# A two-block transformer kernel in float32: the state steps of its RWKV part put in another order

## The reference, cut to what matters

```python
def step(S, inp):
    w_t, k_t, v_t, a_t, b_t = inp[:5]
    sa = jnp.einsum('bhij,bhj->bhi', S, a_t)
    S = S * w_t[:, :, None, :] + sa[..., None] * b_t[:, :, None, :] + v_t[..., None] * k_t[:, :, None, :]
    y = jnp.einsum('bhij,bhj->bhi', S, inp[5]) if emit else None
    return S, y
```

## Time and profile before

| | us |
|---|---|
| median of 3 runs | 2797.05 (2795.35 to 2806.27) |
| profiled execution | 2801.67 |
| its span in the profile | 2799.5 |
| TensorE busy, all of the span | 2506.8 |
| VectorE busy | 894.2 |
| ScalarE busy | 534.8 |
| GpSimd busy | 153.5 |
| mean granted clock of TensorE | 0.937 of full |

### The profile page before, as it was taken

The page is one execution under the profiler, slowest core; times in us unless marked ns, Lnnn a source line. Parts: engine busy times, 40 slices in busy tenths (PEclk is TensorE's granted clock), DMA queues, the critical chain, the costliest instruction groups (busy, mean ns, idle before and its releaser), DMA issues.

```text
span 2799.5 us, 36794 instructions
## 1 busy us (share of the span) xinstructions
PE 2506.8 (90%) x15530; PEld 1778.1 (64%) x15530; DVE 894.2 (32%) x1608; ACT 534.8 (19%) x1067; POOL 153.5 (5%) x145
## 2 busy tenths in 40 slices
PE   8999989999999899999989999999767777777786
PEld 6857678887857788887568888864333343333333
DVE  3733524203725412313575651231111111111112
ACT  2125310001126212002234422121000000000002
POOL 1310000000310000000011110100000000000000
PEclk9999999999999999999999999999888878888778
DMA  8336547545331473453000002559999999999998
GB/s 330 141 135 256 210 181 267 215 151 210 121 144 67 151 273 121 191 230 117 1 1 2 1 2 104 210 203 428 427 427 429 428 428 429 428 429 429 428 429 359
DMA packets 48772, 666.89 MB, mean 238 GB/s; under 512 B 5530, under 2 KB 5573, under 8 KB 7568
## 3 DMA queue, kind: packets, MB, share of 16 engines
q1 hardware_dynamic: 46928, 657.81, 57.7%
q0 software_dynamic: 1728, 7.38, 0.8%
HBM read 664.11 MB, written 1.05 MB: 238 GB/s over the span
## 4 chain that ended last, share of the span: by engine, by line
PE 63%; DMA 27%; DVE 7%; ACT 2%; issue 1%; POOL 0%; DVEq 0%; SPq 0%; ACTq 0%
PE bank L2689 50%; DMA ring<-exp_w 25%; PE bank L2697 6%; PE bank L2701 2%; PE bank L2919 2%; DVE arena L2422 1%; PE bank L1884 1%; DMA ring<-w_in 1%; DVE hT L2566 1%; PE bank L2725 1%; PE bank L1912 1%; DMA arena<-exp_w 1%; ACT arena L2348 0%; PE bank L2939 0%; DVE ring L1441 0%
## 5 line engine op out<-in xcount | busy, mean ns | idle before, releaser
L2689 PE MATMUL bank<-hT,ring 128*128 128x256 f32 (+2 forms) x3232 | 735.2, 387 | 5.2 <-ACT hT L2222 4.0
L2689 PEld LDWEIGHTS bank<-hT,ring 128*128 128x128 f32 x3232 | 603.5, 191 | 139.9 <-issue 63.6
L2697 PE MATMUL bank<-ring,arena 128*32 128x512 f32 (+1 forms) x2496 | 320.9, 655 | 170.6 <-DMA ring<-exp_w 156.9
L2689 PE MATMUL bank<-arena,ring 128*128 128x256 f32 x1600 | 352.7, 381 | 7.1 <-POOL arena L2189 2.8
L2689 PEld LDWEIGHTS bank<-arena,ring 128*128 128x128 f32 x1600 | 304.8, 191 | 50.5 <-POOL arena L2189 3.6
L2697 PEld LDWEIGHTS bank<-ring,arena 128*32 128x32 f32 x2496 | 86.8, 128 | 356.8 <-issue 200.3
L2689 PEld LDWEIGHTS bank<-vec,arena 128*128 128x128 f32 x1344 | 173.2, 208 | 73.2 <-issue 68.4
L2689 PE MATMUL bank<-arena 64*128 64x128 f32 (+4 forms) x1156 | 205.2, 375 | 4.6 <-DVE ring L1441 1.6
L1625 DVE COPY arena<-bank 128x512 f32<-128x512 f32 x64 | 44.3, 692 | 477.9 <-PE bank L2697 477.9
L2697 PE MATMUL bank<-arena 128*32 128x256 f32 (+1 forms) x1568 | 156.7, 541 | 42.0 <-DMA arena<-exp_w 41.5
L2689 PE MATMUL bank<-vec,arena 128*128 128x32 f32 (+2 forms) x1344 | 178.6, 284 | 3.4 <-DVE arena L2422 3.4
(11 more groups left out here) (323 smaller groups left out, 2048.7 us busy)
## 6 DMA issues: line engine op xcount, KB each, us to landing
ring<-exp_w SPq DMA_DIRECT2D x125, 2048.0 KB, 26.2
arena<-exp_w SPq DMA_DIRECT2D x66, 2048.0 KB, 26.0
ring<-w_in SPq DMA_DIRECT2D x38, 2048.0 KB, 7.8
ring<-ada_w SPq DMA_DIRECT2D x24, 2048.0 KB, 7.9
ring<-w_mlp_up SPq DMA_DIRECT2D x16, 2048.0 KB, 7.8
ring<-w_mlp_down SPq DMA_DIRECT2D x16, 2048.0 KB, 7.9
ring<-mod_w SPq DMA_DIRECT2D x12, 2048.0 KB, 7.8
ring<-w_out SPq DMA_DIRECT2D x6, 2048.0 KB, 7.9
```

Source lines behind the costliest of these rows:

```text
L2689: mm = nc.tensor.matmul(out_, a, b, start=(i == 0), stop=(i == len(pairs) - 1))
L2697: mm = nc.tensor.matmul(o, a, b, start=(i < 4), stop=(i >= len(pairs) - 4))
```

## The change

- `keep_busy` goes from U0 (two products in each second U0 of groups 0 to 2, one in each first U0). In U it now stands in every second step, in that of group 3 too.
- U0 is cut in two: U0a with the eight score products, and U0 with the eight state products, added on top in the same banks. U0a is issued some jobs ahead, in banks taken before their turn (`started_early`).
- Y is cut likewise: Ya (state and RK products) ahead of the wait for U, Y (RB products) behind it. In S the kT products are issued ahead of the wait for U.
- BK of a group moves from the next group's state steps into its own solve, behind levels 3 and 4 (not for group 0). S0 of the first chunk moves to level 4, and U0a and U0 of the first chunk stand ahead of W6.
- lora of the next group moves from behind NT to behind the second spread (not for group 0). Widening stands ahead of Ya, S and Y of the second chunk.
- S stands ahead of Y, and the last Y frees two weight slots in place of the last S.

```diff
     for g in range(4):
-        if old:
-            yield "S0", q, 0
-        if g >= 2:
-            yield "BK", q, 0
+        yield "NT", g, 0
+        yield "NT", g, 1
+        if g == 0:
+            yield "mix", "ctx", 8
+            yield "lora", n
         if g == 1:
             yield "BK", q, 0
-        if old:
-            yield "U0", q, 0
             yield "BK", q, 1
-        if new:
-            yield "pick", g
         if old:
             yield "U", q, 0
+            yield "U0a", q, 1
+            if q >= 2:
+                yield "Ya", q, 0
+            yield "S", q, 0
+            yield "S0", q, 1
+            if q >= 2:
+                yield "Y", q, 0
+        yield "pick", g
+        if old:
+            yield "U0", q, 1
+        yield "spread", g, 0
+        if old:
+            yield "U", q, 1
+        yield "spread", g, 1
+        if old and ahead:
+            yield "lora", n
+        for tile in range(4):
+            yield "widen", g, tile
+        if g == 0:
+            yield "mix", "ctx", 10
         if old:
             if q >= 2:
+                yield "Ya", q, 1
+            yield "S", q, 1
             if q >= 2:
                 yield "Y", q, 1
...
+            if g and lev < 5:
+                yield "BK", g, lev - 3
+            if lev == 4:
+                yield "S0", g, 0
+        yield "U0a", g, 0
+        yield "U0", g, 0
         for ci in range(2):
             yield "W6", g, ci
...
+    yield "U0a", 3, 1
     yield "U", 3, 0
-    yield "Y", 3, 0
+    yield "Ya", 3, 0
     yield "S", 3, 0
     yield "S0", 3, 1
+    yield "Y", 3, 0
     yield "gates2", 0
     yield "U0", 3, 1
     yield "gates2", 1
     yield "U", 3, 1
+    yield "Ya", 3, 1
     yield "gates2", 2
+    yield "S", 3, 1
     yield "Y", 3, 1
-    yield "S", 3, 1
     yield "gates2", 3
...
+            def started_early(key):
+
+                n = jobs.at[key][0]
+                assert done[0] <= n < done[0] + BANKS
+                emptied(pe, jobs.order[n - BANKS])
+                return bank[n % BANKS]
...
+                elif what == "U0a":
+                    vt = values_of(g, at[0])
+                    banks = [started_early(("U0", g, at[0], par)) for par in range(2)]
+                    emptied(pe, ("AK", g, at[0], 1))
+                    for p in range(CT):
+                        for par in range(2):
+                            nc.tensor.matmul(banks[par][:, p * 64:(p + 1) * 64], score_of("AK", 2 * at[0] + par)[:, p],
+                                             vt[:, p, pars[par]], start=(p == 0), stop=False)
                 elif what == "U0":
                     banks = paired(what, g, at[0])
-                    if g < 3 and at[0] == 1:
-                        keep_busy(banks[0], 2)
-                    elif at[0] == 0:
-                        keep_busy(banks[0], 1)
-                    emptied(pe, ("AK", g, at[0], 1))
                     pe.wait_ge(state_scaled, 2 * g + at[0] + 1)
                     for p in range(CT):
+                        mms = [nc.tensor.matmul(banks[par][:, p * 64:(p + 1) * 64], ops[0][pars[par], p, tok],
+                                                state_in[pars[par], p], start=False, stop=(p == CT - 1)) for par in range(2)]
```

More of the change, by code:

```diff
@@ L302, in rwkv_steps @@
     for g in range(4):
-        q, n, new, old = g - 1, g + 1, g < 4, g > 0
+        q, n, old = g - 1, g + 1, g > 0
         ahead = n < 4
-        if old:
-            yield "S0", q, 0
-        if g >= 2:
-            yield "BK", q, 0
-        if new:
[L310 to L315, removed]
+        yield "NT", g, 0
[3 more added lines that the diff above has]
+            yield "lora", n
         if g == 1:
             yield "BK", q, 0
-        if old:
-            yield "U0", q, 0
             yield "BK", q, 1
-        if new:
-            yield "pick", g
         if old:
             yield "U", q, 0
-        if new:
-            yield "spread", g, 0
+            yield "U0a", q, 1
[18 more added lines that the diff above has]
+            yield "mix", "ctx", 10
         if old:
             if q >= 2:
[L329 to L343, removed]
+                yield "Ya", q, 1
+            yield "S", q, 1
             if q >= 2:
                 yield "Y", q, 1
-            yield "S", q, 1
         if ahead:
@@ L571, in second_block @@
                 for par in range(2):
-                    add((what, g, *at, par), "v")
+                    last = (what, g, *at, par) == ("Y", 3, 1, 1)
+                    add((what, g, *at, par), "v", [("hold", 0, 2), ("hold", 0, 3)] if last else [])
             elif what == "U0":
@@ L583, in second_block @@
             elif what == "W" or what == "S":
-                last = (what, g, *at) == ("S", 3, 1)
-                add((what, g, *at), "v", [("hold", 0, 2), ("hold", 0, 3)] if last else [])
+                add((what, g, *at), "v")
             elif what == "XT6":
@@ L1729, in paired, with values_of @@
                 return [start((name, g, ci, par), par) for par in range(2)]
+            def started_early(key):
[3 more added lines that the diff above has]
+                return bank[n % BANKS]
+            def values_of(g, ci):
+                cc, _ = chunk_tokens(g, ci)
+                return ar(R_VT + 1024 * (g // 2), TT, CT, P)[:, cc]
             def gates(i):
@@ L1888, in second_tensor @@
                     b = start((what, g, *at))
-                    if g < 3 and at[0] == 1:
+                    if at[0] == 1:
                         keep_busy(b, 1)
@@ L1897, in second_tensor @@
                     finish(mm)
[L1898 to L1901, removed]
+                elif what == "Ya":
+                    _, tok = chunk_tokens(g, at[0])
+                    vt = values_of(g, at[0])
+                    banks = [started_early(("Y", g, at[0], par)) for par in range(2)]
                     emptied(pe, ("RK", g, at[0], 1))
[L1903 to L1920, removed]
                     for p in range(CT):
@@ L1924, in second_tensor @@
                                 part = pars[par]
-                                a, c = ((btT[:, p, part], solved_u[:, par, p]), (ktT[:, p, part], vt[:, p, part]))[i]
-                                mm = nc.tensor.matmul(b[part, p * 64:(p + 1) * 64], a, c, start=(i == 0), stop=(i == 1))
+                                a, c = ((state_in[part, p], ops[3][part, p, tok]),
+                                        (vt[:, p, part], score_of("RK", 2 * at[0] + par)[:, p]))[i]
+                                nc.tensor.matmul(banks[par][part, p * P:(p + 1) * P], a, c, start=(p == 0 and i == 0), stop=False)
+                elif what == "Y":
+                    banks = paired(what, g, at[0])
+                    emptied(pe, ("U", g, at[0]))
+                    for p in range(CT):
+                        mms = [nc.tensor.matmul(banks[par][pars[par], p * P:(p + 1) * P], solved_u[:, par, p],
+                                                score_of("RB", 2 * at[0] + par)[:, p], start=False,
+                                                stop=(p == CT - 1)) for par in range(2)]
+                    for mm in mms:
+                        finish(mm)
+                elif what == "S":
+                    vt = values_of(g, at[0])
+                    btT, ktT = (turned_operands(at[0])[:, i] for i in range(2))
+                    b = start((what, g, *at))
+                    emptied(pe, ("kT", g, at[0]))
+                    for p in range(CT):
+                        for part in pars:
+                            nc.tensor.matmul(b[part, p * 64:(p + 1) * 64], ktT[:, p, part], vt[:, p, part], start=(p == 0), stop=False)
+                    emptied(pe, ("U", g, at[0]))
+                    for p in range(CT):
+                        for par in range(2):
+                            mm = nc.tensor.matmul(b[pars[par], p * 64:(p + 1) * 64], btT[:, p, pars[par]], solved_u[:, par, p],
+                                                  start=False, stop=(p == CT - 1))
                     finish(mm)
```

14 lines of the change are left out of this document (1 added, 13 removed).

## The result

| | before | after |
|---|---|---|
| median of the runs (us) | 2804.8 (7 runs) | 2785.5 (7 runs) |
| ratio, 95% interval | | 0.9932 (0.9918 to 0.9946) |
| profiled execution | 2801.67 | 2785.61 |
| its span | 2799.5 | 2783.8 |

What follows compares the result with a forecast made beforehand. TensorE's work was taken to bound the RWKV part; keep_busy 8.1, U0 7.0, waits 1.4 and 0.5, less a new wait 1.6, gave 15.4 us won: 2786 us profiled, 2781.6 as median, range 2775 to 2792.5.

Steps and rivals of the forecast that it cites:

- U0 split: Score and state products of U0 run grouped instead of in turn: 0.88 us for each of eight U0, 7.0 us won.
- keep_busy out: Net nine keep_busy products leave TensorE's queue, booked at 0.9 us each: 8.1 us won.
- Where such a product only filled a wait, the wait stays: Caveat on removed keep_busy products: the second U0 waited for the scaled state, and that wait would not go with them.
- The rival that had the clock: Four to six more clock falls at 1.5 us each, leaving a gain of 6 to 9 us; chance 0.20.
- Waits that go: TensorE waits before NT, U0 and Y vanish, 1.4 us; small ones before second U0 and BK, 0.5 us.
- The new wait in group 3: Without lora there, TensorE waits before group 3's widening, right behind the last spread: 1.6 us lost.
- One fall after as before: The sum counts one clock fall with TensorE busy, 1.5 us, in the changed kernel as in the old.
- It is hidden: Second U0's wait for the scaled state, about 1.35 us, is covered by pick, or by Y and pick.
- Margin of the scan behind the sigmoids: On ScalarE, the sigmoids queued behind the moved lora end 0.9 us before the scan's first operation.
- BK in the solve at nothing: BK moved into the solve keeps its turns and evictions and delays no X: no time booked.
- the tail within the transfer: At the end, gates2's weight chunk lands 7.7 us after its request, within 8.5 us of work: fits by 0.7 us.
- Y and S split at nothing: Cutting Y into Ya and Y, and S into halves, keeps the number of alternations: no time booked.

## Why the prediction was right, point by point

The forecast was 15.4 us won; the profiles show 15.7, the runs 19. The median came out at 2785.5 us and not 2781.6, because the kernel before measured 2804.8 over seven runs where the forecast started from 2797.05 over three. The total is right. Not all of its working is, and that the errors cancel is luck.

The clock's part is best seen in all seven kernels of the first experiments:

| order | U0 | keep_busy in U0 | recurrence (us) | of it at 1.2 GHz |
|---|---|---|---|---|
| old | alternating | yes (before) | 333.6 | 17 |
| old | alternating | no | 353.1 | 72 |
| old | grouped | yes | 323.8 | 10 |
| old | grouped | no | 316.6 | 14 |
| new | alternating | no | 350.0 (a long execution) | 68 |
| new | grouped | yes | 323.0 | 10 |
| new | grouped | no (after) | 317.8 | 17 |

- **U0 split, 7.0 us: right, and it was more than a term.** 2.87 against 3.72 us, 6.8 us in eight; the kernel before with this edit alone won 7.5 us. The reading that an alternation has its price was right. The Trainium skill, page TensorEngine Tiling (Array Packing), section Key Properties, says that a change of tiling mode drains the engine; the trace agrees as far as the 0.85 us a U0 goes. That a drain is what the 0.85 us are is not shown.
- **keep_busy out, 8.1 us: right in size, wrong as a term by itself.** The nine products less are 8.6 us from start to start: the products that went cost some 0.95 us each, the ones that stay 0.88, so the 8.5 us that the prediction first read from its rows was nearer than the 8.1 it booked. But the sum added the term as if it were free of the others. Taken out of the kernel before, ten of them cost 18 us instead of giving 8; taken out behind the grouping they give 7.2. The step that failed is the sentence "Where such a product only filled a wait, the wait stays", with its silence on the clock. The rival that had the clock put four to six short falls on the new order, and they did not come. What makes the clock fall is the alternating U0 without keep_busy beside it, in either order: 68 and 72 us at 1.2 GHz, against 10 to 24 in the ten kernels with a grouped one. An alternating U0 in the new order with keep_busy was not run. What of an alternating U0 does it (that its records leave gaps, or which part of the array they use) the runs don't show.
- **Waits that go, 1.4 and 0.5 us: right** (1.4 and 0.3 measured), and the W waits became 0.9 us shorter besides.
- **The new wait in group 3, 1.6 us: right, 1.74. What follows it was missed:** a fall of 2.9 us in Ya, S and Y, in both profiles of the changed kernel.
- **One fall after as before: right only in the sum.** The clock is low for 17 us in either profile. But the fall at 1560 us is gone, the one in group 1 is half as long (3.4 us at 1.2 GHz in place of 6.8), and the new one in group 3 takes 6.8.
- **"It is hidden", of the wait for the scaled state: wrong.** It waited 0.46 and 0.92 us. The 1.35 us that I gave the three operations became 2.7 to 3.1, because GpSimd's additions ran beside them; before, they ran earlier. I had placed the masks against pick and not asked what the additions behind them share. The Trainium skill, page SBUF — State Buffer, section Who interferes with whom, says that a vector instruction with two SBUF inputs contends with a GpSimd instruction that reads SBUF. The trace agrees: 0.80 to 1.37 us with two such inputs in place of 0.43, and 0.42 with one.
- **Margin of the scan behind the sigmoids, 0.9 us: right**, no wait. But S takes over a bank of theirs and waited 0.57 and 0.29 us, which I had not looked up.
- **BK in the solve at nothing, the tail within the transfer: right.** No new wait before W, none before gates2.
- **Y and S split at nothing: right.** Ya, S and Y take 4.75 us at the full clock (group 2), Y and S before took 4.74.
- **The order of the jobs: nearly nothing.** The old order with the grouping and without the products has a recurrence of 316.6 us, the changed kernel 317.8, or 314.9 without its fall. The new order, which is most of the diff, costs 1.2 us as it stands and would be worth 1.7 without the fall. With the two small edits that keep the additions and the last spread out of the way (312.1) it is worth 4.5.

Of the 15.8 us, then: U0's grouping 6.8, the nine products 8.6, waits gone or shorter 2.6 (0.32, 0.31, 0.78, 0.3 before the second U0, 0.9 before W), the fall at 1560 us 1.5. Against them: new waits 4.0 (1.74, 1.38, 0.86) and the fall in group 3 2.9. That makes 12.6. The rest are pieces of work of the same count that take less from start to start: BK 1.1 (0.87 in place of 1.02 us where it stands behind T), W and XT 1.0 (most of it the shorter low stretch in group 1's first XT, 5.29 in place of 6.05), T 0.8 and U 0.4, which closes the sum to 0.1 us. Why T and U are cheaper in their new places I did not test. The sum had left out 1.4 us of waits for the scaled state, 0.9 for the sigmoids' banks and 1.4 of the larger fall in group 3, and it had left out gains of about as much.

## What to carry to other kernels

Two matmul shapes that use the array differently should be issued in two runs, not in turn, and the run that needs nothing new goes ahead of the wait: here that one edit won 7.5 us, and made 7 us of filler products needless. A filler that holds the clock up can't be priced by its own duration: take it out together with what makes it necessary, and look at the granted clock, not at the idle time. And when a vector operation moves, look at what GpSimd reads in its new place.

## What the runs showed of the hardware

- A TensorE queue that never runs empty can still be put to 1.2 GHz: with U0 alternating in the changed kernel, W6 and XT6 took 6.71 us in place of 4.02 behind it, 28 us after the last wait.
- The same jobs can keep or lose the clock: the changed kernel's order gave a fall in group 3 in both of its profiles (7.68 us in place of 4.75 for Ya, S and Y), and none in the one profile of the kernel that differs from it by when GpSimd adds.
- 0.43 us of VectorE became 0.80 to 1.37 us beside a GpSimd addition, with both inputs in SBUF, and stayed 0.42 with one of them in PSUM. GpSimd's four additions paid 0.34 us.
- The Trainium skill, page TensorE: Matmul & The Clock Gate, Part 4, says that transposes don't count as busy in the way of products, which had made falls behind T and BK a rival. In the kernels with a grouped U0 none stood behind the turns beside the light products. The one fall that begins right behind turns, in group 0, stands between waits of 2.8 and 1.2 us and is there in the kernel before too, so the runs give the rule no support and do not refute it.
